# Second attention of a two-layer decoder: key blocks that begin at multiples of 128 positions

## The reference

```python
N_META, BLOCK = 16, 128
B_HEADS, B_NOPE, B_ROPE, B_V = 16, 64, 32, 64
...
    k_pos = jnp.arange(L)
    def attend_block(args):
        qn, qp, b = args
        q_pos = N_META + b * BLOCK + jnp.arange(BLOCK)
        s = (jnp.einsum('bqhd,bshd->bhqs', qn, k_nope)
             + jnp.einsum('bqhd,bsd->bhqs', qp, k_pe)).astype(jnp.float32)
        s = jnp.where(k_pos[None, :] <= q_pos[:, None], s, NEG_INF)
        p = jax.nn.softmax(s, axis=-1).astype(v.dtype)
        return jnp.einsum('bhqs,bshd->bqhd', p, v)
```

## Time and profile before

| what | value |
|---|---|
| time, median of 3 runs | 3594.17 us (3593.21 to 3595.28) |
| span of the profiled execution, first to last instruction | 3588.6 us |
| PE busy | 3236.8 us, 90% of the span |
| POOL busy | 1850.7 us, 52% |
| DVE busy, ACT busy | 1767.2 us (49%), 1272.8 us (35%) |
| mean granted clock of TensorE, as a share of full speed | 0.951 |

### The profile page before, as it was taken

How to read it: one execution, slowest core, us unless ns; L and a number is a source line. 1 busy time by engine, 2 the same in 40 slices (tenths; PEclk the granted TensorE clock), 3 DMA queues, 4 the chain that set the end, 5 groups by cost and what they waited for, 6 DMA issues and landing times. The chain is left out here.

```text
span 3588.6 us, 57550 instructions
## 1 busy us (share of the span) xinstructions
PE 3236.8 (90%) x20001; PEld 2506.3 (70%) x20001; DVE 1767.2 (49%) x3672; ACT 1272.8 (35%) x2673; POOL 1850.7 (52%) x1443
## 2 busy tenths in 40 slices
PE   6999997996999995997999999999997996999960
PEld 4788885785888884996566666666655876888850
DVE  3555555675443334663555555455534653433316
ACT  2444444222222323443443444444343222223212
POOL 2555553343344432444788888988872223444412
PEclk8999999997999997997999999999998998999975
DMA  2010003543998965886121011022004438999817
GB/s 99 26 39 33 32 33 86 190 152 112 366 317 303 304 210 193 266 267 167 32 51 38 24 51 48 10 51 51 7 13 166 152 123 287 365 320 310 300 65 322
DMA packets 358657, 536.55 MB, mean 150 GB/s; under 512 B 82897, under 2 KB 278773, under 8 KB 351556
## 3 DMA queue, kind: packets, MB, share of 16 engines
q1 hardware_dynamic: 331492, 457.86, 39.8%
q0 software_dynamic: 26976, 76.27, 5.5%
HBM read 397.39 MB, written 145.38 MB: 151 GB/s over the span
## 5 line engine op out<-in xcount | busy, mean ns | idle before, releaser
L2064 POOL TENSOR_TENSOR ab_acc<-ab_acc,ab_pT 128x1024 f32<-128x1024 f32 (+2 forms) x320 | 654.3, 2045 | 136.1 <-ACT ab_pT L2098 103.2
L2098 ACT ACTIVATE ab_pT<-ab_S 128x512 f32<-128x512 f32 (+4 forms) x704 | 376.3, 537 | 574.7 <-PE ab_S L2172 360.3
L2114 DVE TENSOR_REDUCE ab_mx<-ab_W 128x2 f32<-128x1024 f32 (+5 forms) x352 | 347.1, 994 | 400.7 <-PE ab_W L2187 270.7
L1264 POOL DMA_INDIRECT scratch_y<-ex_y,ex_prow x64 | 64.7, 1011 | 490.5 <-issue 353.3
L2221 PE MATMUL ab_O<-ab_pT,ab_v 128*64 128x512 f32 (+4 forms) x1408 | 304.8, 549 | 0.0
L2170 PE MATMUL ab_S<-ab_q_hi,ab_k_hi 97*128 97x512 f32 (+3 forms) x704 | 292.5, 415 | 1.4 <-DVE ab_q_hi L2126 0.7
L1434 PE MATMUL ex_G<-ex_xT,ex_wg 128*128 128x160 f32 x2048 | 291.7, 301 | 2.1 <-DMA ex_wu<-in_moe_w_up 2.1
L1434 PE MATMUL ex_U<-ex_xT,ex_wu 128*128 128x160 f32 x2048 | 288.6, 299 | 0.0
L1434 PEld LDWEIGHTS ex_G<-ex_xT,ex_wg 128*128 128x128 f32 x2048 | 280.0, 190 | 7.3 <-issue 3.6
L1434 PEld LDWEIGHTS ex_U<-ex_xT,ex_wu 128*128 128x128 f32 x2048 | 281.7, 190 | 0.0
L2171 PE MATMUL ab_S<-ab_q_lo,ab_k_hi 96*128 96x512 f32 (+3 forms) x704 | 261.6, 372 | 0.0
(11 more groups left out here) (308 smaller groups left out, 7105.8 us busy)
## 6 DMA issues: line engine op xcount, KB each, us to landing
ex_wg<-in_moe_w_gate SPq DMA_DIRECT2D x64, 1024.0 KB, 7.0
ex_wu<-in_moe_w_up SPq DMA_DIRECT2D x64, 1024.0 KB, 10.9
ex_wd<-in_moe_w_down SPq DMA_DIRECT2D x64, 1024.0 KB, 12.2
pb_y<-scratch_y SPq DMA_DIRECT2D x17, 1024.0 KB, 7.2
pr_o<-scratch_oT SPq DMA_DIRECT2D x33, 512.0 KB, 4.9
scratch_h<-pr_h SPq DMA_DIRECT2D x33, 512.0 KB, 5.0
scratch_xn<-pr_xn SPq DMA_DIRECT2D x33, 512.0 KB, 2.7
fi_y<-scratch_y SPq DMA_DIRECT2D x16, 1024.0 KB, 14.0
```

What stands on the lines that cost most here:

```text
L2064: nc.gpsimd.tensor_tensor(to, to, pT[0:r, U % RING, :, 0:n], ALU.add).then_inc(added, 1)
L2098: nc.scalar.activation(pT[0:r, U % RING, h, 0:n], S[0:r, h, 0:n], ACT.Exp, scale=B_SCALE).then_inc(exped, 1)
L2114: nc.vector.reduce_max(mx[:, :, t, c:c + 1].rearrange("p h a -> p (h a)"), W[:, j % 2, :, 0:n], AX.X).then_inc(emptied, 1)
```

## The change

A key block is now 128 consecutive positions beginning at 128 b, meta keys included. A group of 512 queries, at positions 16 + 512g and up, then needs the blocks 0 to 4g+4: widths 512 for b up to 4g, then 400, 272, 144, and 16 for the last block, which holds 16 keys. The blocks run in rising order. The number of units and the table `work` stay as they are. The score matmuls of the last block have 16 keys as stationary operand, and the causal mask stands on five blocks instead of four. The values are stored in the new blocks, for which each tile's store is cut into a part of 112 rows for block t-1 and a part of 16 rows for block t, and each head's load of values becomes two DMAs (blocks 0 to 15, and 16 rows of block 16).

```diff
@@ combine_and_project_b, sync @@
-                        sp.dma_start(dram["v"].rearrange("h p t d -> t p h d")[tile_at(j)].rearrange("a p h d -> (a p) h d"),
-                                     v[:, j.slot, :].rearrange("p (h d) -> p h d", d=HD)).then_inc(v_out[j.slot], 16)
+                        values = v[:, j.slot, :].rearrange("p (h d) -> p h d", d=HD)
+                        blocks = dram["v"].rearrange("h p t d -> t p h d")
+                        if j.turn is None and j.c == 0:
+                            pieces = [(blocks[0][0:META // 2], 0, META // 2), (blocks[0][META // 2:META], META // 2, META)]
+                        elif j.turn is None:
+                            pieces = [(blocks[j.c - 1][META:P], 0, P - META), (blocks[j.c][0:META], P - META, P)]
...
+                        for to, at, end in pieces:
+                            sp.dma_start(to, values[at:end]).then_inc(v_out[j.slot], 16)
...
@@ attention_b @@
-            units += [(p, g, b) for b in [*range(1, 4 * g + 5), 0]]
+            units += [(p, g, b) for b in range(4 * g + 5)]
...
-        def first_tile(U):
-            p, g, b = units[U]
-            return max(4 * g + 1, b)
-
         def width(U):
             p, g, b = units[U]
-            return P * (4 * g + 5 - first_tile(U))
+            return 512 - max(0, P * (b - 4 * g) - META)
 
         def depth(U):
-            return P if units[U][2] > 0 else META
+            p, g, b = units[U]
+            return P if b < 4 * g + 4 else META
...
+                def load_v(p):
+                    b = p % 2
+                    for h in range(2):
+                        sp.dma_start(v[:, b, h, 0:NT - 1, :], dram["v"][2 * p + h, :, 0:NT - 1, :]).then_inc(v_in[b], 16)
+                        sp.dma_start(v[0:META, b, h, NT - 1, :], dram["v"][2 * p + h, 0:META, NT - 1, :]).then_inc(v_in[b], 16)
...
-                    n, at = width(U), P * first_tile(U)
-                    kb = slice(META + P * (b - 1), META + P * b) if b else slice(0, P)
+                    n, r = width(U), depth(U)
+                    at = P * (4 * g + 5) - n
+                    kb = slice(P * b, P * b + r)
...
-                    diagonal = b >= 4 * g + 1
+                    diagonal = b >= 4 * g
+                    skip = META if b == 4 * g else 0
+                    m = min(n, P - skip)
...
-                        to, qs = S[:, h, 0:n], slice(at, at + n)
+                        to, qs = S[0:r, h, 0:n], slice(at, at + n)
...
-                            last = nc.tensor.matmul(S[:, h, 0:P], identb[:, :], maskT[:, :], start=False, stop=True)
+                            last = nc.tensor.matmul(S[0:r, h, 0:m], identb[:, 0:r], maskT[:, skip:skip + m], start=False, stop=True)
```

More of the change, by code:

```diff
@@ L1580, in step @@
                         sp.wait_ge(v_dve, j.count(1, 1))
-                        sp.dma_start(dram["v"].rearrange("h p t d -> t p h d")[tile_at(j)].rearrange("a p h d -> (a p) h d"),
-                                     v[:, j.slot, :].rearrange("p (h d) -> p h d", d=HD)).then_inc(v_out[j.slot], 16)
+                        values = v[:, j.slot, :].rearrange("p (h d) -> p h d", d=HD)
[4 more added lines that the diff above has]
+                            pieces = [(blocks[j.c - 1][META:P], 0, P - META), (blocks[j.c][0:META], P - META, P)]
+                        else:
+                            pieces = [(blocks[bass.ds(j.n - 1, 1)].rearrange("a p h d -> (a p) h d")[META:P], 0, P - META),
+                                      (blocks[bass.ds(j.n, 1)].rearrange("a p h d -> (a p) h d")[0:META], P - META, P)]
+                        for to, at, end in pieces:
+                            sp.dma_start(to, values[at:end]).then_inc(v_out[j.slot], 16)
                     k = i.back(3)
@@ L1596, in _ @@
                     sp.wait_ge(k_out[b], 48 * n)
-                    sp.wait_ge(v_out[b], 16 * n)
+                    sp.wait_ge(v_out[b], 32 * n)
                     sp.wait_ge(q_out[b], 16 * n)
@@ L1680, in step @@
                         if j.after(2):
-                            act.wait_ge(v_out[j.slot], j.uses * 16)
+                            act.wait_ge(v_out[j.slot], j.uses * 32)
                         nc.scalar.copy(v[:, j.slot, 0:512], B[:, 6, :]).then_inc(v_act, 1)
@@ L1772, in step @@
                         if j.after(2):
-                            dve.wait_ge(v_out[j.slot], j.uses * 16)
+                            dve.wait_ge(v_out[j.slot], j.uses * 32)
                         nc.vector.tensor_copy(v[:, j.slot, 512:D], B[:, 7, :]).then_inc(v_dve, 1)
@@ L2002, in load @@
                         sp.wait_ge(summed, PU * (p - 1))
-                    for h in range(2):
-                        sp.dma_start(v[:, b, h, :, :], dram["v"][2 * p + h]).then_inc(v_in[b], 16)
+                    load_v(p)
                 oT = dram["oT"].rearrange("(n r) d -> r n d", r=P)
@@ L2019, in _ @@
                 load_first(1)
-                for h in range(2):
-                    sp.dma_start(v[:, 0, h, :, :], dram["v"][h]).then_inc(v_in[0], 16)
+                load_v(0)
                 for g in range(2, NG):
@@ L2216, in attend @@
                     if U == opens[p, g]:
-                        pe.wait_ge(v_in[p % 2], 32 * (p // 2 + 1))
+                        pe.wait_ge(v_in[p % 2], 64 * (p // 2 + 1))
                         if G >= 2:
```

## The result

The changed kernel takes **3559.3 us** (median of 4 runs, 3552.9 to 3560.4) where the kernel before, with a fourth run added to the three above, takes 3593.7 (3588.7 to 3595.3): ratio 0.9905, 95% interval 0.9891 to 0.9919. It is 34 us, about 1%, faster. I had forecast 56.6 us and 3537.6, so the direction was right and some 22 us are missing; the time lies 1.3 us above my range.

A forecast was written before the change was run, and what follows sets the result against it. PE was taken to bound the second attention; 55.7 us for 32 groups plus 1.3 less 0.4 at the tail gave 56.6, so 3594.2 - 56.6 = 3537.6 us, range 3528 to 3558.

The forecast's parts named there:

- the cover of the waits: Second attention: waits at the narrow units are covered by scans and attends and POOL stays hidden, so they cost nothing.
- The sizes, 1.74 us a group: Each of 32 groups: score saves 1.46 and attend 0.88, less 0.45 and 0.15 added; net 1.74 us, 55.7 in all.
- I take 0.45 us: Cost on PE of the new 16-key unit's score, 8 matmuls of 16 columns, between bounds of 0.24 and 0.74 us.
- for the switch of shapes: Some 0.1 us for changing matmul shapes, given with the 0.45 us of the new narrow score.
- a sign of being wrong that I had named: Listed sign against the forecast: the narrow unit's small matmuls start 0.1 us apart.
- 0.94 and 0.83: Attend savings in us when the old last unit went with a 128-wide unit, or with the next group's 512.
- The 0.15 for the wider units: Added PE time a group for 16 more columns in three units: 0.05 us in attends, 0.10 in score.
- PE feeds everybody and waits for next to nothing: Bound of the second attention: PE is full and waits for POOL's sum only twice, 1.5 us together.
- unless a wait grows into the hole: Condition in the second attention: what leaves PE's queue leaves the time, if no new wait fills its place.
- the clock falls: Rival: pauses at each group's end halve PE's clock for 2 us, losing 32 us in all, 3569; chance 0.03.
- The next group's first score waiting for ACT: Listed sign against the forecast: after a narrow unit, PE's first score of the following group waits for ACT.
- The tail: Stage's end after the last unit: 1.3 us gained by the shorter POOL add, less 0.4 in the last pair.

The follow-up runs named there:

- a6_again: Changed kernel with ACT's casts of the next pair begun at unit 6 instead of unit 4, run again in the third group: 3545.0 us.
- a6_rmask: Changed kernel with casts begun at unit 6 and the narrow unit's mask multiplied in fp32r instead of bf16: 3536.0 us.
- a_raise6: Changed kernel with ACT's casts of the next pair begun at unit 6 instead of unit 4, first run: 3541.6 us.
- a6_attend2: Changed kernel with casts begun at unit 6 and the 16-wide attends issued twice, which changes the result: 3551.6 us.
- b_layout: Kernel before with the change's DMAs alone, two stores for a tile of values and two loads for each head: 3590.9 us.
- a6_twice: Changed kernel with casts begun at unit 6 and the narrow unit's 8 score matmuls issued twice: 3565.9 us.

## Why the prediction was off, step by step

The gain of the profiled executions is 31.5 us against 56.6. Two steps failed: the cover of the waits, and the price of the narrow score and attend. The parts, from the pair lengths:

- **The sizes, 1.74 us a group.** In pairs with nobody waiting (a6_again against before) a pair gains 5.91, 5.63, 5.48, 5.64, 5.51 and 5.65 us, mean 5.64, which is 1.41 a group or 45.1 us for 32: **10.6 short**. The term "I take 0.45 us" for the new score was mis-sized: 0.54 to the next row and 0.11 more in the scan behind it, 0.65 together. The 0.1 "for the switch of shapes" should have been four changes of type at 0.08, as a6_rmask shows; half of the starts were 0.1 us apart, a sign of being wrong that I had named. The 0.11 is no matter of type: the scan takes 0.55 in a6_rmask too, and its cause stays open. The floor that the Trainium skill gives ("TensorE: Matmul & The Clock Gate", section "Wait — 56ns, not 53.3ns?"), which I weighed and put aside, fits the set without type changes (0.22 us, 8 starts of 0.027), and is still not the answer for this kernel. The attend, read in a_raise6's fourth pair, saves 0.76 (1.37 to 0.61) and 0.79 (2.01 to 1.22), not 0.94 and 0.83: I let it shrink by columns to nothing, but a6_attend2 shows 0.12 us for its four starts. At the end of group 0 only 0.61 of the 0.76 reach the pair, because the scan of unit 5 then waits for VectorE's reciprocal. The 0.15 for the wider units was right (the intervals concerned grow by 0.12 to 0.14 in a group).
- **The cover of the waits, "PE feeds everybody and waits for next to nothing" and "unless a wait grows into the hole": 14.3 us short** (984.60 against 970.34). The hole was there, and a wait grew into it. This step took the time out of the range: without the wait it is 3541.6 and 3545.0. I checked the waits at the narrow units and at POOL, and not what else stands in ACT's queue: the cast that waits for a load was late by up to 1.3 us already, and each pair reaches it 2.4 us sooner. 8.3 us are PE's wait; the rest goes with the clock, at 0.50 for 6.8 us in each of two pairs.
- **The rival "the clock falls"** (0.03) came true in part and by another road. I looked for it at the pauses of each group's end and found no wait over 0.4 us there; it fell at the load's wait. Its sign in my list, a granted clock below 1.00 inside a pair, was the right one to name. "The next group's first score waiting for ACT" came close: it was that group's second score, unit 6, and for another reason.
- **The first pair** gains 2.4 us and not 5.6: **3.2 short**, which I had not looked at on its own. It has two scans for each of its first units, and VectorE sets their pace. Unit 13 there (after):

```profile
1744.90 4.12 DVE L2124 TENSOR_REDUCE ab_mx<-ab_W 128x2 f32<-128x800 f32 x4 [1.90 <-PE ab_W L2200]
...
1746.04 0.70 PE L2200 MATMUL ab_W<-ab_k_hi,ab_q_hi 96*128 96x512 f32 x2 [0.28 <-DVE ab_mx L2124]
...
1747.17 0.58 PE L2200 MATMUL ab_W<-ab_k_hi,ab_q_hi 96*128 96x384 f32 x2 [0.43 <-DVE ab_mx L2124]
```

  The 0.71 us that the narrow score saves here are waited for VectorE: unit 13 takes 3.51 us, 3.46 before. Another 1.6 us go to the clock at 1731 to 1735 (unit 9 takes 7.55 us, 5.95 before):

```profile
1731.00:1733.00 2.00, 1.93 (x8) 0.83 (x10) 1.98 (x3) 0.00 (x0) 2.00 (x1) 0.68 0.13 40
1733.00:1735.00 2.00, 2.00 (x6) 0.24 (x2) 0.42 (x3) 0.00 (x0) 0.04 (x1) 0.50 0.28 91
```

  The edit to the casts leaves those of the first pair where they were, and the pair stays at 140.7 to 141.1 us: unit 9 is back at 5.95 in a6_again, and the clock is at 0.50 for 3.4 us in units 13 and 14 instead. The fp32r mask takes it to 139.5. Every profiled execution of a changed kernel has one such fall in this pair, and none of the four of kernels with the old blocks has one. PE has gaps there in both, and why the clock falls only after the change stays open; no run tests it.
- **The tail**: I put 1.3 - 0.4. From the last score to the last row of the divide it is 2.2 us after and 5.7 before, and the whole account leaves 2.7 for the tail: 1.8 more than forecast. Some 0.4 of that is the divide at full clock (its starts lie 0.49 us apart instead of 0.91), 0.2 a pause at group 2's narrow unit of 0.16 instead of 0.4, and 1.0 is my booking: of the 1.7 that I took off as the group's own gain only 0.7 lies behind the last score. The short add took 0.24 us, as reckoned (0.25).
- **Right, as forecast**: stage pb, full in the same stretch, with SP's wait for qT down, further than to the 0.4 us a step of the forecast, to

```profile
SPq L1596 <- DVE pb_qT L1794: 0.7, 4, 0.2
```

  from the 12.8 us of the earlier trace rows; POOL 98.94 us a pair (99 forecast) and hidden; the extra loads of v (b_layout: nothing).

Account: 56.6 - 10.6 - 14.3 - 3.2 + 1.8 = 30.3, and 1.2 lie elsewhere in this execution (0.4 before the first score, 0.5 between the divide's last row and VectorE's last instruction, 0.4 behind that): 31.5. With the wait and the type change taken away the kernel needs 3536.0, close to the forecast of 3537.6; that is by an added edit and does not make the forecast's working right. A slip in its own bounds changes nothing here: the best case of 63.7 us leaves out the 0.4 of the tail, 63.3 by its own terms.

## What to carry to other kernels

When PE gets faster, walk the in-order queues of the engines that serve it and look for instructions that wait for a *load*: here the load kept its time while everything around it moved forward, and a short wait in the old list grew. Price such a wait above its length if PE stands still behind it (here 1.7 times, 14.3 for 8.3 us, and 2.8 times, 42.7 for 15.4), and put work that depends on a load some units later than it could first run, which cost nothing here. For matmuls of a few columns count starts and changes of type, not columns.

## What was unexpected of the hardware

- Changing between fp32r and bf16 costs PE about 0.08 us each time on small matmuls: 8 of them take 0.54 us with four changes, 0.38 with two and 0.22 with none.
- Same-type matmuls of 16 x 16 start 0.03 us apart, fp32r too, and 16-wide attends with 64 stationary columns cost the same for each record.
- The granted clock fell to 0.50 at waits of PE of 2.10 and 1.90 us and not at one of 1.94 in the same execution; once it fell 0.84 us behind 16 matmuls of 16 x 16 with no wait shown (a6_twice), and stayed there for 20.5 us while PE was full.
- One unit's shift of a cast, 43 us: 31.1 us of ACT waiting became 15.4 of PE waiting and 27 more that go with the slow clock.
